# First block's attention of a two-block kernel: units of scores taken in pairs, the V product between the turns of two units, four buffers of probabilities

## What is computed

```
sc = einsum('bhqd,bhkd->bhqk', q_blk, k) * scale        # 8 heads, 96 wide, 1024 x 1024 scores
p = softmax(sc)
o = einsum('bhqk,bhkd->bhqd', p, v)                       # v is 64 wide
...
y_a = (o_a * silu(z_a)) @ w_attn_proj
y_f = (fourier(u_f) * silu(z_f)) @ w_fourier_proj
m = sigmoid(g_a + b0) * y_a + sigmoid(g_f + b1) * y_f
x = x + m @ w_out
```

## Time and profile before

| what | value |
|---|---|
| median of 3 runs | 2594.45 us (2590.34 to 2595.15) |
| the profiled execution's own time | 2594.3 us |
| its span | 2592.5 us |
| mean granted TensorE clock | 0.987 |
| PE busy | 2470.2 us, 95% of the span |
| DVE, ACT, POOL busy | 55%, 32%, 15% |
| attention of the first layer, first score matmul to first unit matmul | 214.47 to 449.88 us |
| the same in the second layer | 1096.22 to 1332.32 us |

### The profile page before, as it was taken

One profiled execution on the slowest core, in us unless ns is written; L12 is line 12 of the kernel. 1 busy time (PEld: TensorE's weight loads), 2 busy tenths in 40 slices (PEclk: granted clock), 3 DMA queues, 4 the chain that ended last, 5 costly groups with the idle time before them and its releaser, 6 DMA issues.

```text
span 2592.5 us, 30752 instructions
## 1 busy us (share of the span) xinstructions
PE 2470.2 (95%) x12425; PEld 1809.0 (70%) x12425; DVE 1419.3 (55%) x2274; ACT 836.0 (32%) x1478; POOL 390.0 (15%) x491
## 2 busy tenths in 40 slices
PE   7999998999999999999989999999999989889997
PEld 6857887788777787688868887776556545644553
DVE  2356777342223343477753322234789999777762
ACT  3344545231113142454451311131442103333341
POOL 0014320100000001233110000000325672300000
PEclk9999999999999999999999999999999999999998
DMA  5010000311113211000011111124000011200000
GB/s 204 29 49 1 2 1 4 89 45 44 45 39 130 65 70 44 33 1 2 1 53 38 49 49 49 57 98 137 35 10 33 4 39 41 98 17 33 17 23 26
DMA packets 106382, 116.83 MB, mean 45 GB/s; under 512 B 20705, under 2 KB 78785, under 8 KB 106241
## 3 DMA queue, kind: packets, MB, share of 16 engines
q1 hardware_dynamic: 105088, 110.66, 13.7%
q10 hardware_dynamic: 1152, 4.19, 0.4%
HBM read 96.82 MB, written 16.84 MB: 44 GB/s over the span
## 4 chain that ended last, share of the span: by engine, by line
PE 84%; DVE 9%; ACT 3%; POOL 2%; issue 1%; SPq 1%; DMA 1%; DVEq 0%; POOLq 0%; ACTq 0%
PE PS L656 7%; PE PS L659 7%; PE PS L662 7%; PE PS L597 6%; PE PS L488 5%; PE PS L621 4%; PE PS L1038 4%; PE PS L607 4%; PE PS L799 4%; PE PS L709 2%; PE PS L722 2%; PE PS L533 2%; PE PS L728 2%; PE PS L725 2%; PE PS L1009 2%; DVE R2a L2135 2%
## 5 line engine op out<-in xcount | busy, mean ns | idle before, releaser
L656 PE MATMUL PS<-hHi,R2bR 128*128 128x512 f32 x768 | 301.5, 393 | 7.3 <-POOL hHi L2328 7.3
L659 PE MATMUL PS<-hLo,R2bR 128*128 128x512 f32 x768 | 300.8, 392 | 0.0
L662 PE MATMUL PS<-hHi,R2bR 128*128 128x512 f32 x768 | 300.6, 391 | 0.0
L1826 DVE TENSOR_TENSOR R2bR<-W,R2bR 128x1024 fp32r<-128x1024 f32 x48 | 61.9, 1312 | 267.8 <-ACT R2bR L1354 267.7
L656 PEld LDWEIGHTS PS<-hHi,R2bR 128*128 128x128 f32 x768 | 145.3, 189 | 39.7 <-POOL hHi L2328 9.0
L1419 ACT ACTIVATE R3a<-PS,pT 128x512 f32<-128x512 f32 x64 | 42.3, 687 | 403.6 <-PE PS L662 403.5
L1805 DVE TENSOR_REDUCE negm<-PS 128x1 f32<-128x1024 f32 x128 | 156.5, 1223 | 27.7 <-PE PS L597 22.1
L1370 ACT ACTIVATE R2b<-PS,negm 128x1024 f32<-128x1024 f32 x128 | 142.3, 1112 | 78.4 <-DVE negm L1805 78.4
L799 PE MATMUL PS<-hT,W 128*128 128x512 f32 x384 | 167.1, 596 | 0.0
L662 PEld LDWEIGHTS PS<-hHi,R2bR 128*128 128x128 f32 x768 | 145.3, 189 | 30.3
L659 PEld LDWEIGHTS PS<-hLo,R2bR 128*128 128x128 f32 x768 | 145.2, 189 | 30.1
(11 more groups left out here) (389 smaller groups left out, 4906.6 us busy)
## 6 DMA issues: line engine op xcount, KB each, us to landing
W<-in_w_in SPq DMA_DIRECT2D x10, 2048.0 KB, 8.5
W<-in_w_in SPq DMA_DIRECT2D x33, 512.0 KB, 4.7
xres<-R SPq DMA_DIRECT2D x3, 4096.0 KB, 18.0
W<-in_w_out SPq DMA_DIRECT2D x6, 2048.0 KB, 7.8
R<-xres SPq DMA_DIRECT2D x2, 4096.0 KB, 18.0
R<-in_x ACTq DMA_DIRECT2D x8, 512.0 KB, 7.8
W<-in_w_in SPq DMA_DIRECT2D x4, 1024.0 KB, 6.9
R3a<-rsums SPq DMA_DIRECT2D x16, 256.0 KB, 5.4
```

What stands on the lines that cost most here:

```text
L656: mm = pe.matmul(o, wHi[c % 2][:, k, :], hHi[:, k, ns], start=(k == 0), stop=False)
L659: mm = pe.matmul(o, wHi[c % 2][:, k, :], hLo[:, k, ns], start=False, stop=False)
L662: mm = pe.matmul(o, wLo[c % 2][:, k, :], hHi[:, k, ns], start=False, stop=(k == 7))
```

## The change

- Step p of the new loop takes the pair u = 2p, u + 1. On PE: scores(u + 2), scores(u + 3), p_turn(u), the V product of units u - 2 and u - 1, the q/k turns of the step, p_turn(u + 1). DVE and ACT follow the same steps: DVE both maxima, then the second halves of both units' P copies; ACT both exponentials, then the first halves.
- Pb and PT have four buffers each: two in R2b, two in slot 0 of W, and for the last eight units in R0, where q lay.
- Turns of probabilities and of q/k share a ring of the banks 4, 5 and 7, in the order in which they are made (`turn_plan`).
- q/k turns are one for a step for the heads 2 to 7 (steps 2 to 25), for head 1 two in step 1 and two in step 2.
- `head_out` and the work on h stand at the start of a step, ahead of both maxima or exponentials, once a step. Five rows of h are rounded in the attention instead of four.
- W's slot 0 is released to SP at the first turn of unit 57, not at the Fourier matmuls ahead of the attention.
- The staging of q and k on POOL waits for ACT's copies of the head before, not for PE's turns.
- The y products: first all products of rounded parts of the four banks, then the wait for `s_yback`, then the plain ones.

```diff
-    return [1, 2, 3, 5] if h == 1 else [NT * (h - 1) + n for n in (-1, 1, 3, 5)]
-
-
-QK_TURNS = {u: (h, i) for h in range(1, H) for i, u in enumerate(qk_steps(h))}
-
-
-def turn_bank(h, i):
-    return 4 + i if h == 0 else 7
+    return [1, 1, 2, 2] if h == 1 else [4 * h - 6 + i for i in range(4)]
+
+
+QK_TURNS = {p: [(h, i) for h in range(1, H) for i in range(4) if qk_steps(h)[i] == p] for p in range(UNITS // 2)}
...
+def turn_plan():
+
+    ring, plan, n = (4, 5, 7), {}, 0
+    for p in range(UNITS // 2):
+        fills = [("p", 2 * p, j) for j in range(2)] + [("qk", *x) for x in QK_TURNS[p]]
+        for f in fills + [("p", 2 * p + 1, j) for j in range(2)]:
+            plan[f] = (ring[n % 3], n // 3)
+            n += 1
+    assert n % 3 == 0
+    return plan, n // 3
+
+
+TURNS, N_TURNS = turn_plan()
...
-        Pb = [R2b[:, 0, :], R2b[:, 1, :]]
-        PT = [R2b[:, 2, :], R2b[:, 3, :]]
+        def Pb(u):
+
+            if u % 4 < 2:
+                return R2b[:, u % 4, :]
+            home = W[:, 0, :] if u < UNITS - NT else r0
+            return home[:, (u % 4 - 2) * 1024:(u % 4 - 1) * 1024]
+
+        def PT(u):
+
+            if u % 4 < 2:
+                return R2b[:, 2 + u % 2, :]
+            home = W[:, 0, :] if u < UNITS - NT else r0
+            return home[:, (2 + u % 2) * 1024:(3 + u % 2) * 1024]
...
-                        if j == g == 0:
-                            mm.then_inc(w_used[0], 1)
...
+                def turn(o, fill, src):
+
+                    b, n = bk.turn(*fill)
+                    pe.wait_ge(free[b], n)
+                    for j in range(4):
+                        mm = pe.transpose(PS[:, b, j * P:(j + 1) * P], src(j), ident[:, :])
+                        if fill == ("p", UNITS - NT + 1, 0) and j == 0:
+                            mm.then_inc(w_used[0], 1)
+                    mm.then_inc(full[b], 1)
+
+                def turned(*fill):
+                    b, n = bk.turn(*fill)
+                    pe.wait_ge(free[b], n + 1)
...
-                    pe.wait_ge(free[2 * (u % 2)], bk.count(2 * (u % 2)))
-                    for j in range(2):
-                        o = begin(4 + j)
-                        for k in range(4):
-                            c = 4 * j + k
-                            mm = pe.transpose(o[:, k * P:(k + 1) * P], Pb[u % 2][:, c * P:(c + 1) * P], ident[:, :])
-                        mm.then_inc(full[4 + j], 1)
-                    pt_count.append((bk.count(4), bk.count(5)))
+                    pe.wait_ge(free[2 * (u % 2)], p_count[u])
+                    for i in range(2):
+                        turn(None, ("p", u, i), lambda j: Pb(u)[:, (4 * i + j) * P:(4 * i + j + 1) * P])
...
-                    if t == 1:
+                    if t == 0:
                         begin(6)
-                    pe.wait_ge(free[4], pt_count[u][0])
-                    pe.wait_ge(free[5], pt_count[u][1])
+                    for e in range(2):
+                        for i in range(2):
+                            turned("p", u + e, i)
...
                 scores(0)
-                for u in range(UNITS + 1):
-                    if u + 1 < UNITS:
-                        scores(u + 1)
-                    if u >= 2 and u % 2 == 0:
-                        pv_pair(u - 1)
-                    if u in QK_TURNS:
-                        qk_turn(*QK_TURNS[u])
+                scores(1)
+                for p in range(UNITS // 2 + 1):
+                    u = 2 * p
+                    if u + 2 < UNITS:
+                        scores(u + 2)
+                        scores(u + 3)
                     if u < UNITS:
                         p_turn(u)
+                    if p >= 1:
+                        pv_pair(u - 2)
+                    if u < UNITS:
+                        for x in QK_TURNS[p]:
+                            qk_turn(*x)
+                        p_turn(u + 1)
+                bk.attention()
...
+                    groups = [(br, n, 4 * n + br) for br in range(2, 4) for n in range(2)]
+                    last, first = {}, True
+                    for br, n, b in groups:
+                        o = begin(b)
+                        whole = all(m <= Y_LAST[j] for j in range(4 * (br - 2), 4 * (br - 1)))
+                        for j in range(4 * (br - 2), 4 * (br - 1)):
+                            if m <= Y_LAST[j]:
+                                wh, hi, lo = y_weights_hi(l, m, j, j + 1), yHi[j], yLo[j]
+                                ns = slice(n * 512, (n + 1) * 512)
+                                mm = pe.matmul(o, wh, hi[:, ns], start=(b not in last), stop=False)
...
+                        if whole:
+                            mm.then_inc(full[b], 1)
                     if m > 2:
                         pe.wait_ge(s_yback, l * 12 + y_back(m))
...
+                    for br, n, b in groups:
+                        x = [oT, fT][br - 2]
+                        rest_ = [j for j in range(4 * (br - 2), 4 * (br - 1)) if m > Y_LAST[j]]
+                        for j in rest_:
+                            mm = pe.matmul(PS[:, b, :], g[:, 16 + j, :], x[:, j % 4, n * 512:(n + 1) * 512],
+                                           start=(j == rest_[0] and b not in last), stop=(j == rest_[-1]))
+                        if rest_:
                             mm.then_inc(full[b], 1)
...
+                def exponential(u):
+                    b = 2 * (u % 2)
+                    bk.take(b)
+                    act.wait_ge(s_nm, l * UNITS + u + 1)
+                    if u == UNITS - NT + 2:
+                        act.wait_ge(s_stage, (l + 1) * 2 * H - 1)
+                    act.activation(Pb(u), PS[:, b:b + 2, :].rearrange("p a c -> p (a c)"), ACT.Exp,
+                                   bias=negm[:, u:u + 1], accum_out=rsum[:, u:u + 1]).then_inc(free[b], 1)
+
+                def p_copy(u):
+                    b, n = bk.turn("p", u, 0)
+                    act.wait_ge(full[b], n + 1)
+                    act.activation(PT(u)[:, 0:512], PS[:, b, :], ACT.Copy).then_inc(free[b], 1)
...
+                exponential(0)
+                exponential(1)
+                for p in range(UNITS // 2):
+                    u, j = 2 * p, p - (UNITS // 2 - 5)
+                    if j >= 0:
+                        round_h(j)
+                    if j >= 1:
+                        in_place(j - 1)
+                    if u + 2 < UNITS:
+                        exponential(u + 2)
+                        exponential(u + 3)
+                    p_copy(u)
+                    for x in QK_TURNS[p]:
+                        qk_copy(*x)
+                    if p == UNITS // 2 - 1:
+                        b, n = bk.turn("p", UNITS - 3, 1)
+                        act.wait_ge(full[b], n + 1)
                         round_weights(0)
-                    if u in QK_TURNS:
-                        qk_copy(*QK_TURNS[u])
-                    if u // NT + 1 == H:
-                        if 2 <= u % NT <= 5:
-                            in_place(u % NT - 2)
-                        if 1 <= u % NT <= 4:
-                            round_h(u % NT - 1)
+                    p_copy(u + 1)
+                bk.attention()
...
+                def p_copy(u):
+                    b, n = bk.turn("p", u, 1)
+                    dve.wait_ge(full[b], n + 1)
+                    if u == UNITS - NT + 2:
+                        dve.wait_ge(s_stage, (l + 1) * 2 * H - 1)
+                    dve.tensor_copy(PT(u)[:, 512:1024], PS[:, b, :]).then_inc(free[b], 1)
...
+                maximum(0)
+                maximum(1)
+                for p in range(UNITS // 2):
+                    u, j = 2 * p, p - (UNITS // 2 - 5)
+                    if p >= 5 and p % 4 == 1:
+                        head_out(p // 4 - 1)
+                    if j >= 1:
+                        rest_of_h(j - 1)
+                    if u + 2 < UNITS:
+                        maximum(u + 2)
+                        maximum(u + 3)
+                    p_copy(u)
+                    for x in QK_TURNS[p][:-1]:
+                        qk_rest(*x)
+                    p_copy(u + 1)
+                    for x in QK_TURNS[p][-1:]:
+                        qk_rest(*x)
+                bk.attention()
...
-                    if h == 1:
-                        pool.wait_ge(full[4], bk.count(4))
-                        pool.wait_ge(full[5], bk.count(5))
-                    elif h >= 2:
-                        pool.wait_ge(full[7], bk.count(7) - 2)
+                    if h >= 1:
```

145 lines of the change are left out of this document (58 added, 87 removed).

## The result

| kernel | median, us | runs | ratio to before | 95% interval |
|---|---|---|---|---|
| before | 2592.97 | 20 (2589.85 to 2595.35) | | |
| changed | 2597.81 | 20 (2593.39 to 2602.98) | 1.0020 | 1.0014 to 1.0026 |

The changed kernel is 0.2% slower, 4.8 us; forecast were +5.6 us and 2600. The first score matmul to the first unit matmul takes 238.31 and 238.18 us in the two layers, where before had 235.41 and 236.10 (front table): +2.90 and +2.08, forecast +2.8 each. The two profiled executions themselves, 2594.3 and 2597.03, are only 2.7 apart.

What follows compares the result with a forecast made beforehand. TensorE bounds the kernel (84% of the span). Per layer 3.6 (start) + 5.9 (head_out) - 6.7 (last head) = +2.8 us, two layers +5.6: 2594.3 becomes 2599.9, forecast 2600; range 2590 to 2609.

Steps and rivals of the forecast that it cites:

- head_out: Ahead of both maxima it delays PE's second turn by 0.98 us, heads 0 to 5: 5.9 us a layer lost.
- The body: Pairs of units in the attention: 7.03 us again, PE without stall, neither gain nor loss.
- The passage from turn to V product: Seam in front of the V product on PE: bounds nothing and 0.32 us, taken as 0.09.
- free-seam: Rival: turn to V product costs 0, a pair 6.94 without head_out, 2596 us in all; chance 0.15.
- dear-seam rival: Seam at 0.32 gives 2610 us, or the start's waits bring half speed, 2603; chance 0.22 together.
- The start: First steps of each layer's attention: PE loses 4.65 us against 1.0 before, 3.6 a layer lost.
- the 0.95 in front of scores(3): Start: scores(3) need bank 2 and so wait for exponential(1), 0.95 us lost.
- the 0.3 in front of scores(2): Start: PE loses 0.3 us ahead of scores(2).
- The 1.9 of turn(1): Step 0: turn(1) waits for a bank that ACT copies behind exponential(3), 1.9 us lost.
- steps 1 and 2: turn(3) and turn(5) wait for a bank ACT copies and DVE reads: 0.66 us each, and once 0.18.
- The last head: Split and in-place copy of h once a pair: PE loses 2.7 instead of 9.4 us, 6.7 gained.
- The terms at nothing: Slot 0's load of W, the y products and the later wait for s_yback: set at no gain or loss.

Runs made afterwards that it cites:

- e1: Changed kernel with head_out one step earlier on DVE, between its two P copies; 2579.80 us, 0.9947 of before.
- e2: Changed kernel with ACT's P copy of the step's first unit between the two exponentials, not behind both; 2577.42 us, 0.9945 of before.
- e5: Changed kernel with both copies of head_out done twice for heads 0 to 6; 2615.68 us, 1.0088 of before.
- e4: Kernel before with only the last head's rounding of hT, its rest and in-place copy once a pair of units; 2579.38 us, 0.9950 of before.
- e7: Changed kernel with the edits of e1 and e2, and p_turn(0) ahead of scores(2) and scores(3); 2578.35 us, 0.9943 of before.
- e9: e7 with ACT's P copy of unit 0 ahead of the exponential of unit 2; 2578.93 us, 0.9947 of before.
- e10: e9 with the first q/k turn of head 1 in step 0 instead of step 1; 2577.78 us, 0.9944 of before.

## Why the prediction was right

**The sum.** 2597.81 lies in the range, 2 us below the 2600. The difference of the medians, 4.8, agrees with the two stretches of attention, 5.0, less 0.5 for the y products. Part of this is luck: the profiled layers of both kernels had half speed at the start, and at full clock one term of the start is too large by 1 us a layer (below), while head_out was sized too small by 0.66 and the other pairs together too long by 0.67. With both starts at full clock the terms add up to +1.9 a layer, not +2.8.

**The body.** Forecast 7.03, measured 7.00. The passage from turn to V product, a guess between 0 and 0.32, is 0.093 by single starts, the value taken; from scores to V product it is 0.095. The free-seam and the dear-seam rival fall here. The other half of the dear-seam rival, half speed brought by the start's waits, falls by the rows: it is over before the first of these waits. The 0.03 that the pair did gain was not forecast; the new order has one passage less from turns to scores in a pair, which may be it, but no run isolates that.

**head_out.** The mechanism holds from both sides: e1 removes the cause, e2 the link behind it, and e5 doubles it. The size was 0.98 each. Heads 0, 2 and 4 gave 1.01, but heads 1, 3 and 5 gave 1.17 to 1.19, 6.56 in all. DVE's own rows have the difference. For head 0, reciprocal and copies:

```profile
258.11 0.19 DVE L1847 RECIPROCAL sums<-sums 128x8 f32<-128x8 f32 x1
258.22 0.63 DVE L1850 COPY R2a<-PS 64x512 f32<-64x512 f32 x1
258.86 0.69 DVE L1851 COPY R2a<-PS 64x512 f32<-64x512 f32 x1
```

and for head 1:

```profile
287.11 0.19 DVE L1847 RECIPROCAL sums<-sums 128x8 f32<-128x8 f32 x1
287.34 0.68 DVE L1850 COPY R2a<-PS 64x512 f32<-64x512 f32 x1
288.04 0.69 DVE L1851 COPY R2a<-PS 64x512 f32<-64x512 f32 x1
```

The first copy starts 0.23 behind the reciprocal instead of 0.11, and the second 0.70 behind the first instead of 0.64: 0.18 more. Heads 1, 3 and 5 write partitions 64 to 127 of oT, the others 0 to 63. e5 tells the destination from the head: there the first pair of copies writes the half of the head that follows, and the slow start goes with it. Behind head 0's reciprocal the first copy, now to partitions 64 to 127, starts after 0.23, behind head 1's, now to 0 to 63, after 0.11. So the 0.18 belong to a first copy into the upper half; why it starts later stays open.

**The start.** The forecast of 3.6 was met by the profiled first layer, 3.7, with half speed in it; at full clock it is 2.7. The step that failed is the 0.95 in front of scores(3), with the 0.3 in front of scores(2). It was worked out from the earlier trace rows, which lie in a stretch at half speed. There unit 1's scores came late, so the second exponential starts 1.09 behind turn(0) (220.34, 219.25); in e4, at full clock, it starts 0.09 behind it (221.78, 221.69). At full clock both orders wait 1.35 for the first exponential, which cancels, and scores(3) then follow without a wait. Even in the changed kernel's first layer, at half speed, scores(3) wait only 0.17; the wait there is 1.05 in front of scores(2). The 1.9 of turn(1) measured 1.9, and steps 1 and 2 lose 0.73 and 0.89 against 0.66 and 0.84, where before loses 0.86 in its first interval (8.32 less 7.46 of work).

**The last head.** 6.7 forecast, 6.68 measured. e4 shows that doing the work on h once a pair is enough for 6.53 of it. In the changed kernel that gain is larger, and head_out(6) takes 1.08 of it back. The prediction put part of the 9.4 lost before down to half speed; the second layer of before, with the same 9.4 and full clock, shows that this part was nothing.

**The terms at nothing.** The load of slot 0 and the staging by POOL caused no wait of PE. The y products were given nothing and gave 0.5.

**What comes out of it.** The change joined a gain (13 us in two layers) with a loss (13 by head_out) and a smaller loss at the start (5 to 7). Such a gain can be had without the pairs: e4 is 0.5% faster than before. The changed kernel with the stalls gone (e1, e2, e7, e9, e10) comes to the same 2577 to 2580. None of these kernels can be told from another.

## What to carry to other kernels

When the order of several engines is written by hand, follow one item through all the queues behind it: 1.5 us on an engine that is half idle became 1.0 to 1.2 us of TensorE six times a layer, because two maxima, two exponentials and a copy stood behind it; moving it to where its engine waits anyway, or moving the one copy that TensorE wants ahead of one item, removed it whole. When a change has parts, price and run each alone: here the best part was worth 13 us without the others. At the start of a pipeline, a gap filled with later work tends to reopen at the next bank (e7, e10), so count to the first point that both orders share.

## What was not expected of the hardware

- A passage between full-size turns and V products of 64 columns costs 0.30 us there and back, of which only 0.15 lie outside the product's own span; 0.05 and 0.06 of it fall on the second instruction behind the change.
- The matmul behind a plain fp32 product is recorded 0.4 us early (812.93, the next at 813.56 in the changed kernel, where the spacing is 0.23). Stages should be cut at matmuls with like neighbours.
- The same program, in the same stretch, ran at a granted clock of 1.00 in some layers and at 0.89 to 0.91 in others, which is 1.3 to 1.6 us each time. One profile isn't enough for a term of this size.
- Half speed costs nothing where TensorE waits anyway: before's last head took 34.97 with a V product of 3.62 and 34.98 with one of 1.97.
- A 64-partition copy of VectorE starts 0.11 behind a reciprocal when it writes partitions 0 to 63 and 0.23 when it writes 64 to 127 (changed kernel and e5); cause open.
